# PEER second products: joint and low product in turn, multiply-adds over slabs 8 to 118, low middle values by GpSimd between its fetches

## What is computed

```python
def peer_ffn(x, w_query, sub_keys, u_tab, v_tab):      # per block of 128 tokens
    q = (xi @ w_query).reshape(B, T, PEER_HEADS, 2, PEER_HALF)
    s = jnp.einsum('bthcd,cnd->bthcn', q, sub_keys)
    ...                                                 # top 16 of the sums of both halves
    gate = jax.nn.softmax(best, axis=-1)
    h = jax.nn.gelu(jnp.einsum('bthkd,btd->bthk', u_tab[idx], xi), approximate=False)
    return jnp.einsum('bthk,bthkd->btd', gate * h, v_tab[idx])
```

## Time and profile before

| | us |
|---|---|
| median of 3 runs | 2097.45 (2096.34 to 2099.74) |
| the profiled execution | 2098.77 |
| its span, first to last instruction | 2097.0 |
| granted TensorE clock, mean | 0.993 |
| second products of layer 0, of layer 1 | from 545.1, from 1395.8 |

### The profile page before, as it was taken

One profiled execution on the slowest core, in us unless ns is written; L12 is line 12 of the kernel. 1 busy time (PEld: TensorE's weight loads), 2 busy tenths in 40 slices (PEclk: granted clock), 3 DMA queues, 4 the chain that ended last, 5 costly groups with the idle time before them and its releaser, 6 DMA issues. The chain is left out here.

```text
span 2097.0 us, 37760 instructions
## 1 busy us (share of the span) xinstructions
PE 2048.8 (98%) x13979; PEld 1889.4 (90%) x13979; DVE 1626.9 (78%) x3108; ACT 1221.9 (58%) x2557; POOL 1065.9 (51%) x604
## 2 busy tenths in 40 slices
PE   8899999999999999999999999999999999999999
PEld 8789998888999999877999888899999988997888
DVE  8658987785699998666699777659999878557776
ACT  6555577776555555655456777655555555555443
POOL 2217987778577771001698777757777315000000
PEclk9999999999999999999999999999999999999999
DMA  5145665555799998553566555569999856335554
GB/s 173 52 156 170 201 198 174 180 181 182 250 355 359 362 363 270 152 160 120 165 201 192 177 176 178 189 212 350 365 360 363 309 178 218 101 122 171 191 191 151
DMA packets 151095, 451.78 MB, mean 215 GB/s; under 512 B 20720, under 2 KB 25584, under 8 KB 150912
## 3 DMA queue, kind: packets, MB, share of 16 engines
q1 hardware_dynamic: 127936, 381.64, 55.4%
q0 software_dynamic: 22688, 67.72, 8.8%
q10 hardware_dynamic: 288, 0.01, 0.0%
HBM read 439.14 MB, written 9.44 MB: 214 GB/s over the span
## 5 line engine op out<-in xcount | busy, mean ns | idle before, releaser
L250 ACT ACTIVATE hi<-raw 128x1024 fp32r<-128x1024 f32 (+2 forms) x705 | 738.6, 1048 | 401.7 <-PE bank L1494 102.2
L259 POOL TENSOR_TENSOR lo<-raw,hi 128x1024 fp32r<-128x1024 f32 x256 | 620.7, 2430 | 195.6 <-ACT hi L250 195.0
L259 DVE TENSOR_TENSOR lo<-raw,hi 128x1024 fp32r<-128x1024 f32 (+2 forms) x449 | 544.0, 1215 | 178.9 <-ACT hi L250 178.1
L1529 PE MATMUL bank<-pe_middle,hi 128*128 128x384 f32 x2048 | 415.5, 344 | 11.4 <-DVE pe_middle L1842 10.5
L1529 PEld LDWEIGHTS bank<-pe_middle,hi 128*128 128x128 f32 x2048 | 348.1, 189 | 19.2 <-DVE pe_middle L1842 18.6
L1483 PE MATMUL bank<-xx,hi 128*128 128x512 f32 x1176 | 305.9, 399 | 0.0
L1494 PEld LDWEIGHTS bank<-xx,lo 128*128 128x128 f32 x2048 | 269.4, 188 | 13.8
L1494 PE MATMUL bank<-xx,lo 128*128 128x256 f32 x2048 | 280.5, 280 | 0.0
L1534 PE MATMUL bank<-pe_middle,lo 128*128 128x192 f32 x2048 | 266.8, 271 | 0.0
L1534 PEld LDWEIGHTS bank<-pe_middle,lo 128*128 128x128 f32 x2048 | 265.7, 191 | 0.0
L1610 POOL DMA_INDIRECT pe_seen<-pe_aside,pe_picks x128 | 200.6, 1567 | 118.3 <-DVE pe_sums_aside L1855 60.7
(11 more groups left out here) (431 smaller groups left out, 3424.2 us busy)
## 6 DMA issues: line engine op xcount, KB each, us to landing
raw<-in_peer_u SPq DMA_DIRECT2D x256, 512.0 KB, 3.5
raw<-in_peer_v SPq DMA_DIRECT2D x256, 512.0 KB, 5.7
raw<-in_w_gate_up SPq DMA_DIRECT2D x44, 512.0 KB, 4.3
raw<-in_w_in SPq DMA_DIRECT2D x34, 512.0 KB, 4.3
raw<-in_gla_w_in SPq DMA_DIRECT2D x24, 512.0 KB, 4.2
raw<-in_w_down SPq DMA_DIRECT2D x22, 512.0 KB, 4.3
raw<-in_w_query SPq DMA_DIRECT2D x16, 512.0 KB, 3.5
pe_aside<-pe_stage SPq DMA_DIRECT2D x32, 256.0 KB, 4.3
```

Of the source, the lines that this page charges most:

```text
L250: act.activation(k.hi[:, n % RING, at_hi:at_hi + x * e], k.raw[:, n % RAW, 0:x * e], ACT.Copy).then_inc(k.hi_done, 1)
L259: eng.tensor_tensor(k.lo[:, n % RING, at_lo:at_lo + x * e], k.raw[:, n % RAW, 0:x * e], k.hi[:, n % RING, at_hi:at_hi + x * e].bitcast(F32 ...
L1529: pe.matmul(k.bank[V_BANK[c]][:, 0:2 * TD], cols, middle[:, v % 2].rearrange("p s t -> p (s t)"), start=(v == 0), stop=False, skip_group_c ...
```

## The change

- TensorE waits for the low weights of a slab before its first product and takes joint and low product of each of the 8 column groups in turn, in all slabs.
- `PICK_AT` places the 64 multiply-adds from slab 8 to slab 118, 4 in 7 slabs, instead of from 10 to 108, 16 in 25. `MERGE_AT` moves from 115 to 124.
- The subtraction for the low middle values moves from VectorE to GpSimd, for all slabs. GpSimd's queue now runs over the slabs: subtraction for slab v+2, then, if VectorE has mixed a round in its loop's round v-1, one round of fetches, row first and value second.
- The first four rows are fetched ahead of all subtractions, the first four values after the subtraction for slab 2, when the stored values have landed.
- The store of the last eight slabs of values moves from SyncE to ScalarE, directly behind the last gelu, after a wait for it.

```diff
-PICK_AT = {10 + n * 25 // 16: n for n in range(PICKS)}
-MERGE_AT = 115
+PICK_AT = {8 + n * 7 // 4: n for n in range(PICKS)}
+MERGE_AT = 124
...
-                    if 0 <= i < NK and i % STAGED == STAGED - 1:
+                    if 0 <= i < NK - 1 and i % STAGED == STAGED - 1:
                         put_aside(i // STAGED)
...
                     pe.wait_ge(m_lo.sem, m_lo.at(v + 1))
                     pe.wait_ge(k.hi_done, v0 + v + 1)
-                    for part in (range(0, 5), range(5, KD)) if v == 0 else (range(KD),):
-                        for c in part:
-                            if v == 0 and V_BANK[c] < 3:
-                                pe.wait_ge(gated.sem, gated_before(NK - 1 - (NK - 1 - V_BANK[c]) % 3))
-                            high(v, c)
-                        pe.wait_ge(*k.lo_at[v0 + v])
-                        for c in part:
-                            last = low(v, c)
+                    pe.wait_ge(*k.lo_at[v0 + v])
+                    for c in range(KD):
+                        if v == 0 and V_BANK[c] < 3:
+                            pe.wait_ge(gated.sem, gated_before(NK - 1 - (NK - 1 - V_BANK[c]) % 3))
+                        high(v, c)
+                        last = low(v, c)
                     last.then_inc(k.eaten, 1)
...
+                def fetch_value(n):
+
+                    pool.indirect_dma_start(seen[:, n:n + 1], None, aside.rearrange("j i t -> (j i t)").unsqueeze(1),
+                                            bass.IndirectOffsetOnAxis(ap=picks[:, 1, n:n + 1], axis=0))\
+                        .then_inc(picked[n % FOUND].sem, 16)
+
+                def fetch_row(n):
+
+                    pool.indirect_dma_start(found[:, n % FOUND], None, v_rows,
+                                            bass.IndirectOffsetOnAxis(ap=picks[:, 0, n:n + 1], axis=0),
+                                            element_offset=l * NK * NK * D).then_inc(picked[n % FOUND].sem, 16)
+
+                def split_middle(v):
+                    pool.wait_ge(m_hi.sem, m_hi.at(v + 1))
+                    pool.tensor_tensor(middle[:, v % 2, 1], hidden[:, v], middle[:, v % 2, 0].bitcast(F32), ALU.subtract)\
+                        .then_inc(m_lo.sem, 1)
...
                 pool.wait_ge(placed.sem, placed.at(16 * ASIDE))
-                for x in range(2):
-                    pool.wait_ge(written[x].sem, written[x].at(8 * NK // STAGED))
-                for n in range(PICKS):
-                    if n >= FOUND:
-                        pool.wait_ge(mixed.sem, mixed.at(n - FOUND + 1))
...
+                for n in range(FOUND):
+                    fetch_row(n)
+                split_middle(0)
+                split_middle(1)
+                for v in range(NK - 2):
+                    split_middle(v + 2)
+                    if v == 0:
+                        for x in range(2):
+                            pool.wait_ge(written[x].sem, written[x].at(8 * NK // STAGED))
+                        for n in range(FOUND):
+                            fetch_value(n)
+                    n = PICK_AT.get(v - 1)
+                    if n is not None and n + FOUND < PICKS:
+                        pool.wait_ge(mixed.sem, mixed.at(n + 1))
+                        fetch_row(n + FOUND)
+                        fetch_value(n + FOUND)
                 pool.wait_ge(mixed.sem, mixed.at(PICKS))
...
                     last.then_inc(bent.sem, 1)
+                    if i == NK - 1:
+                        b = i // STAGED
+                        act.wait_ge(bent.sem, bent.at(NK))
+                        act.dma_start(aside[:, STAGED * b:, :], stage[:, b % 2]).then_inc(written[b % 2].sem, 16)
...
-                    if i >= NK - 2:
-                        split_middle(i - NK + 2)
                 for v in range(NK):
-                    if v + 2 < NK:
-                        split_middle(v + 2)
                     if v < NK - 2:
                         split_lo(k, dve, v0 + v + RING)
```

More of the change, by code:

```diff
@@ L1838, in apply @@
                                              op1=ALU.mult).then_inc(applied.sem, 1)
[L1840 to L1843, removed]
                 def mix(n):
```

## The result

The changed kernel takes 2281.32 us in the median of four runs (2269.82 to 2287.52), the kernel before 2096.89 in the same measurements: a ratio of 1.087, 95% interval 1.085 to 1.090. The profiled execution took 2269.82 us with a span of 2268.1 us, 171.1 more than before. It is the shortest of the four; two of the others show a granted clock of 0.962 in place of its 0.968, and are 14 us longer at that.

A forecast was written before the change was run, and what follows sets the result against it. TensorE, 98% busy, bounds the kernel; its slab start times decide. Per layer -11.4 + 67 + 5.8 + 7.1 + 1.7 = +70.2, for two +140.4, on 2098.77 us gives 2239.2, as median 2238; range 2130 to 2280.

The forecast's parts named there:

- rival D: Rounds: most subtractions wait for a whole instruction, or the clock drops at stalls there too; 2275 to 2330, chance 0.13.
- A: Second products: GpSimd's queue of fetches and subtractions becomes the bound; 2180 to 2275 us, chance 0.62.
- old stalls gone: TensorE's waits in the two layers' slabs vanish with a freer VectorE: -11.4 us a layer in the sum, at most -22.8.
- The fetches in between: GpSimd's rounds: fetches and subtractions need 20.6 us for 7 slabs, 4.5 above 16.1; 67 us a layer.
- Port meetings: GpSimd's subtractions meet VectorE's two-input instructions two times in three and wait half: 0.42 us each.
- Rival B: Rounds: GpSimd and VectorE hardly hold each other up, only the order is late; 2129, up to 2180 us, chance 0.15.
- The clock: TensorE at the lower clock after idle time at stage end or ahead of slab 3: +1.7 us a layer, shorter stalls nothing.
- VectorE freed: VectorE loses a 0.35 us subtraction a slab, its multiply-adds spread, the merge moves: at most -22.8 us.
- The start of slab 0: Start of a layer's second products: first subtraction, behind four row fetches on GpSimd, ends at 546.25, not 545.05: +1.2 us.
- Slab 3: Start of second products: its subtraction, behind store landing and four value fetches, ends at 557.7, due at 553.2: +4.6 us.
- The end: GpSimd's copy of partial sums stands behind its last subtraction, so merge and joins come late, 858.0 for 850.84: +7.1 us.
- The order of the products and the merge: Slabs: joint and low product in turn cost 0; the merge no longer stands ahead of a split TensorE needs soon.

The follow-up runs named there:

- e4: Changed kernel with each fetch round one slab later, so GpSimd does not wait for its multiply-add: 2219.73 us.
- e9: Changed kernel with one fetch a round from round 4 on, the row alone, the value fetch left out: 2176.92 us.
- e12: Changed kernel with only the row fetched from round 4 on and each round one slab later: 2136.51 us.
- e6: Changed kernel with a round's two fetches behind different subtractions, row two slabs after its multiply-add's slab, value three: 2229.82 us.
- e3: Changed kernel without fetch rounds 4 to 63 and their multiply-adds, all subtractions still on GpSimd: 2112.95 us.
- e10: Changed kernel with eight products of the identity ahead of TensorE's wait in slabs that rounds make late: 2322.43 us.
- e5: Changed kernel with multiply-adds 1 to 63 on 64 of 1024 columns, fetches whole: 2242.58 us.
- e1: Changed kernel with the subtraction back on VectorE and GpSimd's rounds in one queue again, all else kept: 2095.47 us, ratio 0.9993.
- e8: Changed kernel with the subtraction back on VectorE, GpSimd's rounds in one queue and five raw buffers in place of four: 2088.33 us, ratio 0.9947.
- e2: Kernel before with the new order of the products alone: 2096.59 us, ratio 0.9999.

## Why the prediction was right, and where its sizes were off

The direction, the cause and the place were right: 2238 us was forecast, 2281 measured, 140 us of loss against 171 in the profiled execution and 184 in the medians. 2281 is 1.3 us past the end of the range, 2280, and in the band of rival D (2275 to 2330), which had a chance of 0.13, and not in that of A (2180 to 2275). The profiled execution, at 2269.82 us the shortest of the four, was inside. By the terms, both layers together:

| term | predicted, us | in the traces, us |
|---|---|---|
| TensorE waits between slabs, rounds and slab 3 | 143.2 | 137.2 |
| slower clock | 3.4 | 37.4 |
| old stalls gone | -22.8 | -22.8 |
| start of the stage, end of it and what follows | 16.6 | 12.5 |
| sum | 140.4 | 164.3 of 171.1 |

The waits are the sum over the 127 steps from one slab's last joint product to the next one's first, each less its 0.288 us: 68.0 and 69.2. The old stalls are counted whole since these waits are measured from no stall at all. The 6.8 us that are missing lie inside slabs: 94 pairs took between 0.30 and 0.45 us, which the count of slow pairs leaves out, 7.7 us in all. 69 of them are the first pair of a slab behind a wait, so they belong to the stalls.

**The fetches in between (67 us a layer).** The mechanism is what the trace shows, and the size was close: 137.2 less 13.2 for slab 3 are 62 us a layer. 7 slabs from slab 12 to 115 took 21.5 us where 20.6 were forecast, clock drops included. From slab 116 on the pace was 2.34 us, from slab 122 on the forecast 2.29 to 2.30. But the term was built on a wrong picture. I had GpSimd busy without a gap, 17.7 us of work and 2.9 us of waits for VectorE. In fact it waits for multiply-adds (17.3 us of 200) and for ScalarE (16.2): lateness and load act together and neither alone gives the size. Taking the lateness away gains 62 us (e4), half of the load 104 us (e9), both 145 us (e12), and only with the fetches moved apart is GpSimd full (e6). That the hand sum came out near the measurement is partly chance.

**Port meetings.** That GpSimd's and VectorE's two-input instructions wait for each other is seen in the row of 771.97, in e3 against e12 (0.61 and 1.03 us for the same subtraction), and priced at 0.42 us it was near. Rival B, in which they hardly do, falls. The section "Who interferes with whom" of the Trainium skill ("SBUF — State Buffer") states that these instructions contend and that the order of issue decides which engine is blocked. The trace agrees: VectorE's product of 771.97 took 0.56 us in place of 0.15, GpSimd's subtraction 0.93 in the mean in place of 0.61.

**The clock (1.7 us a layer).** This is the step that failed. "For the shorter stalls of the rounds I add nothing" was a choice without a row that bore it out; the stalls of 1 to 2.4 us in the rounds brought drops all through the stage, 19 us a layer. It was named in rival D and not priced in the sum; the mechanism of A and the clock of D came true together. e10 shows the cause. Priced at what it measured, it would have put the forecast at 2272 us; the rest up to the median of 2281 is less than the 11.5 us between the median and the profiled execution, from which the table is read. How many idle times, and of what kind, bring a drop stays open: e4 waits nearly as much in the same 200 us (27.2 us against 34.9) and its clock is 1.00 there, e5 waits 28.5 and has 0.94. The longest single idle time in that stretch is 2.3 us in the changed kernel, 1.9 in e5, 1.8 in e4 and 1.5 in e6, whose clock is 1.00 too.

**VectorE freed.** Sized as a ceiling, and taken whole. In the changed kernel this did no harm, since new waits cover the old. e1 shows that it was no gain to be had by this alone, and e8 that with a fifth buffer a part of it is. What is next in line is late loads and, in e8, still VectorE, where two multiply-adds stand in a row.

**Start and end.** The start of slab 0, +1.2, came out at +0.8. Slab 3, +4.6, came out at 6.6. The store took 9.1 us until the first value fetch, and no run had it back on SyncE's queue. The end, +7.1: the trace of the changed kernel after its last slab shows each step of it.

```profile
929.14 0.60 POOL L1611 TENSOR_TENSOR pe_middle<-pe_hidden,pe_middle 128x192 fp32r<-128x192 f32 x1 [1.70 <-ACT pe_middle L1705]
...
929.68 0.58 POOL L1638 DMA_DIRECT2D pe_hidden<-pe_sums_aside  x1
...
932.74 0.36 PE L1529 MATMUL bank<-pe_middle,hi 128*128 128x384 f32 x1
...
935.97 1.22 DVE L1881 TENSOR_TENSOR h<-h,pe_hidden 64x1024 f32<-64x1024 f32 x1 [6.99 <-DMA pe_hidden<-pe_sums_aside]
...
937.22 1.22 DVE L1881 TENSOR_TENSOR h<-h,pe_sums_aside 64x1024 f32<-64x1024 f32 x1
...
938.48 1.23 DVE L259 TENSOR_TENSOR lo<-raw,hi 128x1024 fp32r<-128x1024 f32 x1
...
939.62 1.67 DVE L1887 TENSOR_TENSOR pe_hidden<-bank,pe_hidden 128x192 f32<-128x192 f32 x6
```

The last joint product starts at 932.74, the joins at 939.62, 6.9 us behind it where they had stood 0.4 us ahead: 7.3. The stretch up to layer 1's first joint product is only 4.5 us longer, so some of that is won back on the way; how wasn't looked into. In e3 and e12 it is 7.6 and 7.2 us longer.

**The order of the products and the merge: 0**, as predicted (e2).

## What to carry to other kernels

An engine with a low busy share is no free place for a step with a due time: ask how long its longest block between two due times is, what that block waits for, and whether it meets the engine that was relieved at a shared port. Price both the lateness of the block and the load, and then the clock: stalls of 1 to 2 us that recur cost a quarter more again here by the clock of TensorE (37.4 us on 137.2), though in e4 and e6, with 37 and 20 slow pairs, only 9 and 5 us. And before a ceiling of gain is put into a sum, look at what is next in line; here it was the loads and the multiply-adds in a row: the relief of VectorE alone brought nothing, a fifth load buffer alone 0.2%, both 0.5%.

## What the runs showed of the hardware

- An indirect fetch on GpSimd takes 0.94 us, and one that starts while VectorE runs an instruction with two operands in SBUF ends 0.82 us after that: so did all 53 fetches that started between 600 and 700 us of the kernel before, to within 0.02 us.
- GpSimd's subtraction of 128 x 192 took 0.60 us, as taken from 128 and 512 columns; up to 1.69 us where it met VectorE.
- A 256 KB store of eight slabs of values landed in 4.3 us (median) from SyncE's queue. The last one of each layer, at the start of the second products, landed in 4.3 and 5.2 us from SyncE's queue in the kernel before (issued at 550.66 and 1401.32) and in 8.3 and 7.3 us from ScalarE's in the changed kernel (545.66 and 1481.46). So it isn't another store that makes the difference; whether it is the queue or the moment, 5 us earlier in layer 0, wasn't tried.
- With idle times of TensorE of up to 2.3 us in the rounds the granted clock was 0.94 in the mean of 640 to 840 us, with them filled (e10) or absent (e3) 1.00; in e5, with idle times of up to 1.9 us, it was 0.94, and in e4 and e6, with up to 1.8 and 1.5 us, 1.00.
